# The second weight sum ahead of the sixth product's result, and one token block fetched early, in a streaming encoder layer

## The reference

```
u = rms_norm(h, norm_pre)
qa, ka, va, za, qg, kg, vg, zg, lr, ga, gg = split_cols(u @ w_in)
oa = attention(qa, ka, va, sinks);   y_a = (oa * silu(za)) @ w_branch_attn
og = gated_linear_attention(qg, kg, vg, lr);   y_g = (rms_norm(og) * silu(zg)) @ w_branch_gla
merged = sigmoid(ga + b1) * y_a + sigmoid(gg + b2) * y_g
h = h + rms_norm(merged @ w_out, norm_post)
```

## Time and profile before

| | |
|---|---|
| median of 3 runs | 2850.39 us (2848.67 to 2850.72) |
| the profiled execution | 2849.08 us, span 2847.3 us |
| TensorE busy, matmuls | 2746.1 us, 96% |
| VectorE busy | 2120.7 us, 74% |
| ScalarE busy | 1205.7 us, 42% |
| GpSimd busy | 78.7 us, 3% |
| transfers | 456.95 MB, mean 160 GB/s |

### The profile page before, as it was taken

One profiled execution on the slowest core, in us unless ns is written; L12 is line 12 of the kernel. 1 busy time (PEld: TensorE's weight loads), 2 busy tenths in 40 slices (PEclk: granted clock), 3 DMA queues, 4 the chain that ended last, 5 costly groups with the idle time before them and its releaser, 6 DMA issues. The chain is left out here.

```text
span 2847.3 us, 52025 instructions
## 1 busy us (share of the span) xinstructions
PE 2746.1 (96%) x20860; PEld 2603.7 (91%) x20860; DVE 2120.7 (74%) x3375; ACT 1205.7 (42%) x1972; POOL 78.7 (3%) x55
## 2 busy tenths in 40 slices
PE   7999999998999999999999999999899999999996
PEld 7999999998999999999777887878799999999996
DVE  7898777778787787777777777787576877655556
ACT  5343333445354333344555566565422322442331
POOL 0221000000000000000000000000000000000001
PEclk9999999999999999999999999999999999999998
DMA  4555333345344333344656565565534555555664
GB/s 152 164 185 177 122 128 127 122 132 209 100 141 142 123 128 128 120 133 133 193 164 187 171 190 177 165 191 167 194 133 170 212 198 198 170 173 184 184 195 138
DMA packets 234186, 456.95 MB, mean 160 GB/s; under 512 B 23904, under 2 KB 139744, under 8 KB 233072
## 3 DMA queue, kind: packets, MB, share of 16 engines
q1 hardware_dynamic: 233968, 453.91, 49.8%
HBM read 365.90 MB, written 88.47 MB: 160 GB/s over the span
## 5 line engine op out<-in xcount | busy, mean ns | idle before, releaser
L2164 PE MATMUL bank<-th,w_hi 128*128 128x272 f32 x2360 | 687.3, 291 | 8.7 <-DVE w_lo L1429 6.4
L2164 PE MATMUL bank<-tl,w_hi 128*128 128x272 f32 x2360 | 682.7, 289 | 0.0
L2164 PE MATMUL bank<-th,w_lo 128*128 128x272 f32 x2360 | 682.0, 289 | 0.0
L2164 PEld LDWEIGHTS bank<-th,w_hi 128*128 128x128 f32 x2360 | 445.2, 189 | 13.1 <-DVE w_lo L1429 8.0
L1416 DVE TENSOR_TENSOR w_lo<-w_raw,w_hi 128x1024 fp32r<-128x1024 f32 x224 | 273.8, 1223 | 239.2 <-ACT w_hi L989 238.8
L1004 ACT ACTIVATE w_hi<-w_more 128x1024 fp32r<-128x1024 f32 x236 | 250.3, 1061 | 469.7 <-DVE w_more L1448 247.8
L2164 PEld LDWEIGHTS bank<-tl,w_hi 128*128 128x128 f32 x2360 | 445.3, 189 | 1.0 <-issue 1.0
L2164 PEld LDWEIGHTS bank<-th,w_lo 128*128 128x128 f32 x2360 | 444.9, 189 | 0.0
L989 ACT ACTIVATE w_hi<-w_raw 128x1024 fp32r<-128x1024 f32 x224 | 236.8, 1057 | 365.9 <-PE bank L2476 228.0
L1429 DVE TENSOR_TENSOR w_lo<-w_more,w_hi 128x1024 fp32r<-128x1024 f32 x236 | 295.1, 1251 | 111.0 <-ACT w_hi L1004 108.8
L2142 PE MATMUL bank<-uh,w_hi 128*128 128x272 f32 x1024 | 317.0, 310 | 13.5 <-DVE w_lo L1416 8.6
(11 more groups left out here) (278 smaller groups left out, 5653.1 us busy)
## 6 DMA issues: line engine op xcount, KB each, us to landing
w_raw<-in_w_tiles SPq DMA_DIRECT2D x344, 512.0 KB, 4.1
w_more<-in_w_tiles SPq DMA_DIRECT2D x120, 512.0 KB, 3.6
p_scratch<-stage SPq DMA_DIRECT2D x44, 544.0 KB, 3.0
gl<-p_scratch SPq DMA_DIRECT2D x24, 512.0 KB, 5.7
w_pair<-in_w_tiles SPq DMA_DIRECT2D x9, 1024.0 KB, 8.7
gate_scratch<-stage SPq DMA_DIRECT2D x16, 544.0 KB, 3.0
gate_scratch<-stage SPq DMA_DIRECT2D x64, 136.0 KB, 4.2
gate_even<-gate_scratch SPq DMA_DIRECT2D x8, 1088.0 KB, 6.8
```

The costliest lines, as they stand in the source:

```text
L2164: ins = pe.matmul(out[:, 0:GAW], wt[:, k], ut[:, k], start=start and k == 0 and i == 0, stop=stop and k == HK - 1 and i == 2, skip_group_c ...
```

## The change

Two edits. The first moves one line in the list of VectorE: the second weight sum for the next pair, sum_weights(n + 1, 2), is called ahead of the wait for the sixth product instead of behind c21. The second gives token block 0 another raw buffer, xs_blocks (the whole of xs) in place of the part of ul0. Its load no longer waits for the first product of pair 29, only for the stores of all eighths, and is issued at n = HELD_AT + HK + 1 = 11. ScalarE, which writes its high part over the old block, waits for that product itself.

```
-        tok_raw = [ul0_raw[:, 0:HK], tl5_raw[:, 2], ul0_raw[:, HK:KT], ...]
+        tok_raw = [xs_blocks, tl5_raw[:, 2], ul0_raw[:, HK:KT], ...]
...
             def load_held(q):
-                sp.wait_ge(s_mp, N_Q * (TURN - 1) + q + 1)
                 if q == 0:
                     sp.wait_ge(s_tst, 16 * HK)
+                else:
+                    sp.wait_ge(s_mp, N_Q * (TURN - 1) + q + 1)
                 ge(sp, s_tld[q % 2], 16 * (q // 2))
...
                 if n + 1 < MIX:
                     load_mix(n + 1, 0)
-                if turn:
+                if n == HELD_AT + HK + 1:
                     load_held(0)
...
                         act.wait_ge(s_tld[t % 2], 16 * (t // 2) + 16)
+                        if t == 0:
+                            act.wait_ge(s_mp, N_Q * (TURN - 1) + 1)
                         act.activation(tok_hi[t], tok_raw[t], ACT.Copy).then_inc(s_thi, 1)
...
+                sum_weights(n + 1, 2)
                 dve.wait_ge(s_mp, N_Q * n + 6)
                 dve.tensor_tensor(c21, s1_buf[n % 2], b_ps, ALU.add).then_inc(s_post, 1)
                 dve.wait_ge(s_post, taken(n, 5))
                 dve.tensor_tensor(c21, c21, r0, ALU.mult).then_inc(s_cm, 1)
                 if n == SUMS_AT:
                     spread(1, MIX_W, bank[6:8], rstd[:, 0:MIX_W])
-                sum_weights(n + 1, 2)
```

More of the change, by code:

```diff
@@ L333, in build_trunk @@
         tok_lo = [ul0[:, 0:HK], tl5[:, 2], ul0[:, HK:KT], tl5[:, 1], tl5[:, 0], tl5[:, 3], tl5[:, 4]]
-        tok_raw = [ul0_raw[:, 0:HK], tl5_raw[:, 2], ul0_raw[:, HK:KT], tl5_raw[:, 1], tl5_raw[:, 0], tl5_raw[:, 3], tl5_raw[:, 4]]
+        tok_raw = [xs_blocks, tl5_raw[:, 2], ul0_raw[:, HK:KT], tl5_raw[:, 1], tl5_raw[:, 0], tl5_raw[:, 3], tl5_raw[:, 4]]
         w_src_of = [w_raw[:, 0], w_raw[:, 1]] + [w_more[:, i] for i in range(4)]
```

## The result

The changed kernel takes 2841.43 us in the median of 11 runs (2838.49 to 2844.77); 11 runs of the kernel before beside them have a median of 2848.97 us. The ratio is 0.9972, 95% interval 0.9964 to 0.9981: 0.28% faster, some 8 us, between 5 and 10. 2842.3 was forecast. The profiled execution took 2838.49 us, the shortest of the eleven, with a span of 2836.7 us; so its 10.6 us less than the span before are partly chance, and the places have to be read one by one.

A forecast was written before the change was run, and what follows sets the result against it. TensorE is busy 96% of the span, so only its waits can be given back. 5.0 us (pairs 5 to 10) + 3.1 (change of group) = 8.1 from 2850.39 gives 2842.3 us median, range 2838.5 to 2847.5.

The forecast's parts named there:

- Pairs 5 to 10: Projection passes where TensorE waits 0.67 us each for w_lo; moving the sum gains 5.0 us, bounds 0 and 6.8.
- The chain: Sixth result, c21 added and scaled, second weight sum, ScalarE's high part, VectorE's low part; the sum's move starts ScalarE 0.83 us earlier.
- the products in these pairs also run slightly slower, which the change does not touch: Pairs 5 to 10: reason given for taking 5.0 us and not the upper bound of 6.8.
- The other pairs: The other 51 pairs of the projection: the chain has time to spare, so gain 0; ordinary pair stays at 21.20 us.
- the reserve: Ordinary pair: low part of product 2's weights is done 1.6 us before TensorE wants it.
- The change of group: Pair 29's end to pair 30's start, TensorE waits 9.1 us; gain 3.1: block 2.3, sum 0.8; bounds 0.8 and 3.1.
- From here VectorE runs without a gap: Change of group, after c22's addition: no VectorE idle up to the second sum, so everything behind is 2.28 us earlier.
- The condition on block 1: Change of group: token block 1 must land by 682.9; forecast 682.6, 2.6 us earlier than before, 0.3 us to spare.
- The first rival: Change of group: remaining transfers close up, block 1 lands at 685, early block brings nothing; 5.8 us gain, 2844.6; chance 0.19.
- The new wait behind c22: Change of group: product 7 of pair 29 waits 0.9 us for c22's addition, at 687.9.
- The slower rival: c21, behind a sum awaiting a late weight block, delays product 2's bank; 2854 us; chance 0.04.
- the second rival: Pairs 5 to 10: VectorE becomes the bound, GpSimd uses up the 0.83; only 3.1 us gained, 2847.3; chance 0.13.

The follow-up runs named there:

- the sum alone: Kernel before with only the second weight sum moved ahead of c21, token block 0 loaded as before: 2841.47 us, ratio 0.9966.
- The two doses: One or two unread 128x1088 VectorE additions ahead of the second sum in pairs 13 to 27, kernel before: pairs last 21.23 and 22.56 us.
- the block alone: Kernel before with only token block 0 loaded early, the second sum behind c21 as before: 2845.99 us, ratio 0.9987.
- the order of the lists: Kernel before, token blocks put behind work wanted sooner on VectorE and ScalarE at the change of token group, without either edit: 2840.84 us, ratio 0.9964.
- change and order: Changed kernel with token blocks put behind work wanted sooner on VectorE and ScalarE at the change of token group: 2833.27 us, ratio 0.9938 to before.

## Why the prediction was right

**Pairs 5 to 10: right in mechanism, a little small.** The chain was the one named: VectorE's idle went from 1.13 to 0.31 us, the six waits went, and the sum alone brings this gain. 5.0 us was forecast, 5.75 measured, within the bounds of 0 and 6.8. The step that was too small is "the products in these pairs also run slightly slower, which the change does not touch". It touches them: their slowness was the late first matmuls of products whose input comes just in time. Pair 5 now lasts 21.21 and pair 6 21.34 us, pair 4 21.20 in place of 21.55, and only pairs 7 to 10 lie at 21.4 to 21.5, as forecast. Cause and size of the remainder were shown with GpSimd's work taken away.

**The other pairs: right.** 21.20 us as before. The two doses bound the reserve from both sides: 1.3 us more costs 0.03 a pair, 2.5 us more costs 1.36. The 1.6 us of the prediction is a little high, since a pair already loses some tenths when the weights come just in time.

**The change of group: the sum about right, its two terms mis-sized.** 3.1 us was forecast; 2.76 and 3.24 in two profiles, by the start of product 3 of pair 30. The parts were put at 2.3 for the block and 0.8 for the sum, and are 1.8 and 1.3; that the two errors cancel is luck. VectorE did start block 0's low part 2.33 us earlier with the block alone (12.35 us behind the start of pair 29, 14.68 before), as said. The step that failed is "From here VectorE runs without a gap": with the block alone it idles 0.50 us for block 1. The sum alone gives 0.83 on the chain and 0.50 besides. In VectorE's list c12 and the low parts at the start of pair 29 stand behind the low part of product 2's weights, and come 0.8 us earlier with it. SyncE asks for block 0 only behind the store of pair 28's result, which waits for ScalarE's tanh of that c12, and for block 1 only behind a weight block that waits for a low part. With the sum moved, block 0 is asked for 4.17 us behind the start of the pair instead of 4.99 (and lands 0.5 us earlier), block 1 at 6.6 instead of 7.4. That is a way by which the first edit acts on the transfers, and I had not seen it.

**The condition on block 1.** It was forecast to land 6.5 us after its issue, needed the 6.9 us or less that I gave it, and landed after 8.0 and 7.1. So the step from 431 GB/s to a landing 2.6 us sooner after the issue failed: it was 1.1 to 2.0 us sooner. The miss cost little. With the block alone VectorE idled 0.50 us for it; in the changed kernel the block was asked for 0.8 us earlier, which the prediction did not have, and VectorE idled 0.38 us for it in the first profile and not at all in the second. The first rival (it lands where it did, nothing is gained by the block) is out, since the block alone gains 1.8 us.

**What came next.** The new wait behind c22 was 0.9 by the forecast and 1.0 and 0.6 in the profiles; 2.4 and 4.6 were forecast for the others, and are 2.2 and 4.4 (with the refilling of TensorE 2.4 and 4.6). The slower rival, c21 behind a late weight block, shows nowhere: no idle time of VectorE ahead of the second sum, and TensorE waits nowhere for c21. Nor does the second rival: VectorE still idles 0.31 us ahead of the low part, and the moved sum keeps its 1.22 us.

**The total.** 8.1 us forecast, 8.5 by the traces of the projection, 8 by the ratio. The rivals at 5.8 and 3.1 us lie outside what the traces show; by the ratio's interval alone (5.4 to 10.3 us) the first could not be excluded.

## What to carry to other kernels

Where two engines hand work to and fro, look for the instruction that the other engine waits for and ask whether something that nobody waits for stands ahead of it; moving it cost nothing here, but it pays only where the chain is met, and one or two doses of idle work per pass tell how far it is from being met. Follow what an earlier instruction releases on the queue of transfers too: here that was worth 0.5 of the 1.3 us that the moved sum gave at the change of group. And before an input is fetched early, order the work that it is waiting among: at this change of group the order of the lists was worth 7.5 us, the early block 1.8.

## What the runs showed of the hardware

GpSimd's square of 128x1088 elements and its additions of 128x544 lengthen VectorE instructions that run beside them and read two operands in SBUF: 1.22 to 2.17 us, 0.43 to 1.17 and 1.59. The Trainium skill, "SBUF — State Buffer", section "SBUF: two separate sides", has a VectorE instruction with two SBUF inputs and a GpSimd instruction that reads SBUF lock each other out for the whole instruction; the runs with 8 columns in place of 544, in which all three return to 1.23, 0.43 and 0.44, agree.

Weights, or a bank, that are ready only at the very moment cost TensorE up to 0.14 us a product without any wait in the profile: pairs of 21.5 instead of 21.2 us.

At the change of group TensorE's granted clock fell to 0.5 in or shortly after waits of 2.1 to 4.4 us, but not after each of them, and stayed there for 3.4 us, or for 6.9. That is so in 12 of the 13 profiles; in the last, change and order, no wait is longer than 0.57 us and the clock stays full. Product 3 of pair 30, behind the third wait, takes 7.11 us at the full clock (with 32 further matmuls counted in), 8.60 before, and 8.59 and 9.45 in two profiles of the changed kernel: 1.5 us more, and 2.3. Such a stretch in the changed kernel, and one before (clock third from the end, half of full speed, which is 1.2 GHz):

```profile
699.00:701.00 2.00, 2.00 (x11) 2.00 (x10) 2.00 (x2) 2.00 (x3) 0.00 (x0) 0.51 0.58 190
```

```profile
708.00:710.00 2.00, 2.00 (x11) 2.00 (x10) 2.00 (x2) 2.00 (x2) 0.00 (x0) 0.50 0.53 172
```

So a wait of 4.4 us costs some 6 with what follows it, and taking the waits away gives both back: from the kernel before to change and order the way from pair 29 to pair 33 is 10.9 us shorter, while the recorded waits in it fall by 8.3 (9.1 to 0.8). The other 2.6 us are the low clock and TensorE's slow first steps behind a wait.
